# Weight pieces split into high and low parts in two halves, with TensorE waiting per half piece

## What is computed

```python
def swiglu(h, w_gu, w_down):
    gate, up = jnp.split(h @ w_gu, 2, axis=-1)
    return (jax.nn.silu(gate) * up) @ w_down
...
x = x + 0.5 * swiglu(rmsnorm(x, ffn1_norm[i]), ffn1_w_gu[i], ffn1_w_down[i])
```

## Time and profile before

| | |
|---|---|
| median of three runs | 3886.77 us |
| the profiled execution's own time | 3886.8 us |
| its span, first to last instruction | 3885.0 us |
| mean granted TensorE clock | 0.958 |
| TensorE busy | 3564.5 us (92%) |
| VectorE busy | 2276.5 us (59%) |
| ScalarE busy | 1839.1 us (47%) |
| GpSimd busy | 606.9 us (16%) |

### The profile page before, as it was taken

One profiled execution on the slowest core, in us unless ns is written; L12 is line 12 of the kernel. 1 busy time (PEld: TensorE's weight loads), 2 busy tenths in 40 slices (PEclk: granted clock), 3 DMA queues, 4 the chain that ended last, 5 costly groups with the idle time before them and its releaser, 6 DMA issues. The chain is left out here.

```text
span 3885.0 us, 45081 instructions
## 1 busy us (share of the span) xinstructions
PE 3564.5 (92%) x18342; PEld 2997.1 (77%) x18342; DVE 2276.5 (59%) x2608; ACT 1839.1 (47%) x2400; POOL 606.9 (16%) x208
## 2 busy tenths in 40 slices
PE   7998799999899996899998799899998789999999
PEld 6887677788778876688887688787878568787887
DVE  4475458776566667656666454555555554555654
ACT  4453257665356562456554244444443344444443
POOL 0001129572042320142400200000000000000000
PEclk9998899999999998899998899999999899999999
DMA  5542046665276752376743035454544115354453
GB/s 217 188 148 87 1 174 239 225 240 204 101 271 233 275 206 106 134 258 238 265 166 131 1 109 189 153 189 149 198 163 164 62 68 194 142 200 157 152 195 136
DMA packets 89978, 653.57 MB, mean 168 GB/s; under 512 B 10032, under 2 KB 10032, under 8 KB 10928
## 3 DMA queue, kind: packets, MB, share of 16 engines
q1 hardware_dynamic: 78768, 573.10, 40.4%
q0 software_dynamic: 11008, 77.60, 5.6%
HBM read 649.61 MB, written 1.05 MB: 167 GB/s over the span
## 5 line engine op out<-in xcount | busy, mean ns | idle before, releaser
L1424 DVE TENSOR_TENSOR w_lo<-raw,w_hi 128x2048 fp32r<-128x2048 f32 x540 | 1421.0, 2636 | 661.0 <-ACT w_hi L1003 660.7
L1003 ACT ACTIVATE w_hi<-raw 128x2048 fp32r<-128x2048 f32 x540 | 1031.0, 1913 | 601.2 <-PE acc L518 410.2
L516 PE MATMUL wrk<-w_hi,h_hi 128*128 128x512 f32 (+1 forms) x2496 | 973.3, 390 | 61.5 <-DVE w_lo L1424 41.4
L518 PE MATMUL wrk<-w_hi,h_lo 128*128 128x512 f32 (+1 forms) x2496 | 956.2, 383 | 0.0
L517 PE MATMUL wrk<-w_lo,h_hi 128*128 128x512 f32 (+1 forms) x2496 | 955.1, 383 | 0.0
L516 PEld LDWEIGHTS wrk<-w_hi,h_hi 128*128 128x128 f32 x2496 | 473.7, 190 | 157.8 <-DVE w_lo L1424 52.3
L2082 POOL TENSOR_TENSOR arena<-arena,c 128x2048 f32<-128x2048 f32 x92 | 492.1, 5356 | 473.1 <-ACT arena L1003 447.1
L518 PEld LDWEIGHTS wrk<-w_hi,h_lo 128*128 128x128 f32 x2496 | 472.9, 189 | 93.3
L517 PEld LDWEIGHTS wrk<-w_lo,h_hi 128*128 128x128 f32 x2496 | 474.0, 190 | 85.2 <-issue 0.2
L516 PE MATMUL acc<-w_hi,hid_hi 128*128 128x512 f32 x1144 | 447.9, 392 | 9.4 <-DVE hid_lo L1507 9.4
L518 PE MATMUL acc<-w_hi,hid_lo 128*128 128x512 f32 x1144 | 445.9, 390 | 0.0
(11 more groups left out here) (254 smaller groups left out, 3501.4 us busy)
## 6 DMA issues: line engine op xcount, KB each, us to landing
raw<-in_wts SPq DMA_DIRECT2D x540, 1024.0 KB, 4.8
arena<-in_mods POOLq DMA_DIRECT2D x72, 1024.0 KB, 5.2
const<-in_const SPq DMA_DIRECT2D x1, 2176.0 KB, 10.1
c<-in_bias POOLq DMA_DIRECT2D x8, 256.0 KB, 3.4
x<-in_x SPq DMA_DIRECT2D x1, 1024.0 KB, 5.3
c<-in_c SPq DMA_DIRECT2D x1, 1024.0 KB, 4.8
out<-x SPq DMA_DIRECT2D x1, 1024.0 KB, 3.9
row<-in_rows SPq DMA_DIRECT2D x1, 512.0 KB, 11.5
```

The costliest lines, as they stand in the source:

```text
L516: nc.tensor.matmul(o, l_h, r_h, start=first, stop=False, skip_group_check=True)
L518: return nc.tensor.matmul(o, l_l, r_h, start=False, stop=last, skip_group_check=True)
L1003: return nc.scalar.activation(o, i, f, **kw)
L1424: tt(w_lo[:, ns % SLOTS, :], raw[:, ns % SLOTS, :], w_hi[:, ns % SLOTS, :].bitcast(F32), ALU.subtract).then_inc(lo_ready, 1)
```

## The change

`hi` and `lo` each issue two instructions of 128 x 1024 for a piece instead of one of 128 x 2048, and `hi_ready` and `lo_ready` count two per piece. TensorE's wait moves from the head of each call to the first product that uses a half (`split(n, part)`). The load of piece n waits until both halves of piece n - 3 are split, as before. `grouped` still waits for the whole piece. The matmuls, their order and the loads are the same.

```diff
             def load(n):
                 if n >= SLOTS:
-                    sp.wait_ge(lo_ready, n - SLOTS + 1)
+                    sp.wait_ge(lo_ready, 2 * (n - SLOTS + 1))
...
+            def split(n, part):
+                pe.wait_ge(lo_ready, 2 * n + part + 1)
...
             def across(ns, o, h_at=None, n_at=None, kc=KC):
-                pe.wait_ge(lo_ready, ns + 1)
                 s = ns % SLOTS
                 for q in range(kc):
+                    if q % 4 == 0:
+                        split(ns, q // 4)
...
                 def gate_up(s, p, t):
                     n = ns + (3 * s - 1 if s else 0) + p
-                    pe.wait_ge(lo_ready, n + 1)
...
                     for q in range(4):
+                        if q % 2 == 0:
+                            split(n, q // 2)
...
                 def down(s, t, half):
-                    pe.wait_ge(lo_ready, n + 1)
                     pe.wait_ge(taken, use[name, f"t{s}"] + 1)
                     for j in range(2):
+                        split(n, j)
...
                 def part(n, t, wait=False):
-                    pe.wait_ge(lo_ready, ns + n + 1)
                     for q in range(4):
+                        if q % 2 == 0:
+                            split(ns + n, q // 2)
...
                 def grouped(ns, kc, k0, width, labels, h_at=None, along_=False):
-                    pe.wait_ge(lo_ready, ns + 1)
+                    split(ns, 1)
...
-                fn(w_hi[:, ns % SLOTS, :], raw[:, ns % SLOTS, :], ACT.Copy).then_inc(hi_ready, 1)
+                for part in range(2):
+                    v = slice(part * PW // 2, (part + 1) * PW // 2)
+                    fn(w_hi[:, ns % SLOTS, v], raw[:, ns % SLOTS, v], ACT.Copy).then_inc(hi_ready, 1)
...
             def lo(ns):
-                dve.wait_ge(hi_ready, ns + 1)
-                tt(w_lo[:, ns % SLOTS, :], raw[:, ns % SLOTS, :], w_hi[:, ns % SLOTS, :].bitcast(F32),
-                   ALU.subtract).then_inc(lo_ready, 1)
+                for part in range(2):
+                    dve.wait_ge(hi_ready, 2 * ns + part + 1)
+                    v = slice(part * PW // 2, (part + 1) * PW // 2)
+                    tt(w_lo[:, ns % SLOTS, v], raw[:, ns % SLOTS, v], w_hi[:, ns % SLOTS, v].bitcast(F32),
+                       ALU.subtract).then_inc(lo_ready, 1)
```

## The result

A ratio compares a kernel's runs with those of the kernel before on the same chip; it lies near the ratio of the two medians, but is not exactly that (at most 0.001 apart).

The account below looks back on a forecast made before the run. TensorE, busy 92% of the span, was taken as the bound. The terms sum to -8.8 us, and with -6.9 of clock to -15.7, taking 3886.8 to 3871.1 us; the range was 3860 to 3893.

Parts of the forecast that it names:

- start: Start of the program: VectorE starts piece 0 1.07 us earlier, taken as -0.9 us because TensorE is at half clock.
- five modulated openings and the clock behind them: Five modulated FFN openings: each TensorE wait loses 1.07 us, -5.3; behind three, the lost clock all returns, -6.9 us.
- delta-net projections: Two mixers: TensorE's 0.19 us wait for `w_lo` at every second piece, 12 times, goes: -2.3 us.
- stick-breaking and sparse mixer; splits in chains: Sparse mixer between -1 and +1, taken as -0.2 us; extra split time ahead of chains in mixers and FFNs, +1.7 us.
- attention: Second attention opening: the piece ahead of `turned_low` ends at 2949.9 instead of 2950.6, -0.6 us.
- GpSimd openings, `ffn2_0`: Opening of `ffn2_0`: the second GpSimd product gets between the halves and delays the second half, +2.1 us.
- `ffn2_1`, and the three like `ffn1_2`: Openings: in `ffn2_1` the first half precedes the product, -2.3 us; in `ffn1_2` and its like a wait goes, -1.25 each.
- steps of `ffn2_0`: Steps where VectorE and GpSimd alternate without pause: 0.15 us for each of 27 pieces, +4.0 us.
- `ffn1_1`, its opening and steps: Opening with the same pattern as `ffn1_2`, -1.25 us; its steps only in the range, up to +10 if drawn in.
- rival B: Whole kernel: waits shrink but the 1.2 GHz stretches stay, 3878 us; chance 0.22.
- rival C: GpSimd products between halves stall TensorE 3.0 us each in mid-piece; with 12 stalls 3907 us, slower; chance 0.15.

Follow-up runs that it names:

- second trace: The changed kernel run once more with no edit, for a second profile: 3900.41 us, ratio 1.004.
- run 1: The changed kernel with pieces split whole in the six FFNs with GpSimd products, halves elsewhere: 3879.42 us, ratio 0.9987.
- run 11: The changed kernel with each GpSimd product cut into four of 128 x 512, back to back: 3873.38 us, ratio 0.9966.
- run 9: The changed kernel with halves only in the first two pieces of FFNs without GpSimd products and in delta-net and attention mixers: 3876.55 us, ratio 0.9982.
- run 6: The changed kernel with whole pieces in `ffn2_0` and `ffn1_1` alone, halves everywhere else: 3879.03 us, ratio 0.999.
- runs 4 and 5: The kernel before and the changed kernel, each with GpSimd products replaced by fills of zeros: 3857.34 and 3847.01 us.
- run 12: The kernel before, whole pieces, with each GpSimd product cut into four of 128 x 512: 3914.53 us, ratio 1.0074.
- run 7: The changed kernel with halves on ScalarE only; VectorE's part is one instruction that waits for both: 3900.95 us, ratio 1.0052.

## Why the prediction was wrong, step by step

Stage by stage, of the profiled executions (us, after minus before; a stage ends with its last update of `x`), by the prediction's own terms. The stages are read from unrounded times and add up to the 7.4 us; the forecast was -15.7:

| term | predicted | measured |
|---|---|---|
| start | -0.9 | longest wait for `w_lo` 12.5 to 11.6; stage -2.2, second trace +0.3 |
| five modulated openings and the clock behind them | -5.3 and -6.9 | five stages: -5.1 |
| delta-net projections | -2.3 | waits gone; two stages -1.6 and +3.1 |
| stick-breaking and sparse mixer; splits in chains | -0.2 and +1.7 | +2.0 and -0.2 |
| attention | -0.6 | -0.8 |
| GpSimd openings, `ffn2_0` | +2.1 | +4.2 |
| `ffn2_1`, and the three like `ffn1_2` | -2.3, and -1.25 each | -1.6, and -0.2, -0.1, +1.4 |
| steps of `ffn2_0` | +4.0 | +4.3 |
| `ffn1_1`, its opening and steps | -1.25 | +4.0 |

**Right.** The sizes of the halves. A met wait costs nothing that these rows show: steps of after, with 16 waits for pieces instead of 8 (the prediction says 12 calls a step; its own count of matmuls, four calls of 12 and four of 6, makes 8), in the chain of waits,

```profile
3207.79 0.44 PE wrk L618 x4
...
3224.57 0.44 PE wrk L618 x4
```

stand 16.78 us apart as before. The start, the attention opening, and the waits of 0.19 in the projections, of which none is left, though the second delta-net mixer as a whole came out longer (below).

**The openings, mis-sized.** Four of the five waits are 1 us shorter, as the earlier trace rows let expect, the fifth is not:

```profile
2715.00 0.47 PE L520 MATMUL wrk<-w_hi,h_hi 128*128 128x512 f32 x1 [2.32 <-DVE w_lo L1436]
...
3703.71 0.47 PE L520 MATMUL wrk<-w_hi,h_hi 128*128 128x512 f32 x1 [2.35 <-DVE w_lo L1436]
```

```profile
2715.10:2721.80 6.70, 6.70 (x23) 5.35 (x24) 3.58 (x4) 1.10 (x2) 0.00 (x0) 0.75 0.71 267
3695.10:3698.50 3.40, 3.40 (x12) 2.74 (x11) 2.46 (x11) 0.00 (x0) 0.00 (x0) 0.50 0.00 0
```

The second fence is two windows. In the first, behind a wait that was 3.3 us, the granted clock is 0.75, where it was 0.50 over 6.7 us: half of the stretch at 1.2 GHz is gone, not all. The nearest rows, the two waits of 2.4 us, did not carry over, though the waits became 2.3. The second window lies in the fifth opening, behind idle time of 2.02 us that the kernel before had too (2.07), at full clock there; it delays the transposes and takes the gain. Behind the first of the three waits, the one of 3.4 us at 0.50, nothing came back (0.59 at 2516.9 to 2520.3). By TensorE's busy time in these stages 2.1 of the 6.9 us of clock came, 0.8 and 1.3, and 1.4 went in the fifth stage. So the openings came nearer to rival B than to the forecast.

**GpSimd openings.** In `ffn1_2` the wait of 1.30 went, as forecast, though because both halves ran ahead of the product and not with the product between them. But "the next one (0.46) about stays" was wrong: DVE, POOL and PE of after,

```profile
1277.35 6.13 DVE L1436 TENSOR_TENSOR w_lo<-raw,w_hi 128x1024 fp32r<-128x1024 f32 x1 [0.46 <-ACT w_hi L1011]
...
1277.77 4.61 POOL L2094 TENSOR_TENSOR arena<-arena,c 128x2048 f32<-128x2048 f32 x1
...
1283.53 0.50 PE L520 MATMUL wrk<-w_hi,h_hi 128*128 128x512 f32 x1 [1.80 <-DVE w_lo L1436]
```

The next product held the first half of the next piece, and the wait for it is 1.80: 1.76 us of waits are now 1.80, and the two FFNs like it fare the same (1.63 to 1.78, 1.75 to 1.79). In the second of these, `ffn1_3`, the granted clock was 0.50 for 3.4 us behind the wait, where it had been full; that is its +1.4. `ffn2_1` did gain, 1.6 us. In `ffn2_0` the product got between the halves as forecast; TensorE waited 3.13 us at 538.29, and behind it the granted clock was 0.50, where before it was full; the 2.1 us did not hold that. The window:

```profile
537.80:541.20 3.40, 2.91 (x7) 2.33 (x8) 3.40 (x5) 0.29 (x1) 0.24 (x1) 0.51 0.71 222
```

**Clock outside the openings.** The forecast had no term for it. The second delta-net mixer is 3.1 us longer, with its idle time as before (43.4 us in both). After, and before:

```profile
2000.60:2305.90 305.30, 261.85 (x1760) 234.15 (x1761) 176.99 (x344) 122.70 (x224) 28.24 (x12) 0.89 0.20 73
...
1990.50:2292.60 302.10, 258.66 (x1760) 230.69 (x1761) 175.61 (x322) 120.95 (x203) 28.25 (x12) 0.90 0.20 74
```

The stick-breaking mixer's +2.0 is of the same kind (1.8 of it busy time). The halves in the mixer do not settle it alone: with the same halves it took 299.8 us in run 1, 300.4 in run 11 and 300.0 in run 9, and 305.3 in both traces of after.

**The steps, where the sign was decided.** The forecast priced one product against one pair of halves, and put only the second instruction's fixed cost (0.15 us for each of 27 pieces) on the path of `ffn2_0`. "The total of GpSimd's time, all that can block, doesn't grow" was the argument against rival C. It is true, and GpSimd's time even fell, but it is the wrong sum. While both engines had work queued they took turns in these stages, one instruction each: a whole piece and a product in 6.7 us before, half a piece and a product in 5.6 us now. VectorE gets half as much done per turn, so a piece takes two turns, some 11 us, while products last. It falls behind, and TensorE is stopped in mid-piece. The +4.3 us of the steps has the size of the forecast, +4.0, by accident: it is mostly two stalls of 3.35 and one wait of 5.95 us where three of 1.5 to 1.6 and one of 3.2 had been, and not 27 times 0.15. `ffn1_1` was held to be safe by VectorE's lead ("up to +10 if `ffn1_1` is drawn in too" was kept in the range only); the lead goes in two turns.

So two steps of the prediction failed. A product against halves was priced at 0.15 us a piece and with `ffn1_1` safe: `ffn2_0` and `ffn1_1` were to take 4.9 us more and took 12.5, of which 9.3 are idle time of TensorE. And all of the 6.9 us of clock was to come back: TensorE's matmul time rose by 7.4 us instead. Of the 23.1 us between forecast and trace, 7.7 lie in these two FFNs, 7.1 in the modulated openings with their clock, 5.6 in the other GpSimd openings and 3.8 in the delta-net mixers. With the two FFNs whole (run 6) the gain is 5.5 us, not the 20.6 that the other terms of the forecast add up to.

**Rival C** is what happened in the two FFNs, and B in most of the rest, with clock lost besides. A stall was priced at 3.0 us and takes 3.35; there are three in steps, not twelve, and the openings and `hid_lo` add to them. The rule of the Trainium skill (SBUF — State Buffer, "Who interferes with whom"), that such a VectorE instruction and a GpSimd instruction that reads SBUF exclude each other, is borne out by runs 4 and 5: with fills, which read nothing of SBUF, no subtraction took over 2.44 us, not even where a fill ran beside it. The same section of the Trainium skill says that issue order decides who blocks; here it was seen not to be enough, since in run 12 a piece stood behind products that started after it.

What stays open: what decides where the granted clock falls, in run 7 above all, and what makes GpSimd give way or not. The 5 us by which the medians of before and after differ more than their profiled executions fit the clock too, without being shown to be it: the six runs of after go from 3894.2 us at a mean clock of 0.956 to 3903.8 at 0.952.

## What to carry to other kernels

Where two engines exclude each other and both have work queued, price an edit per turn and not per instruction: cutting one engine's instruction in two halves what it gets per turn, unless the other's are cut as well. Here the same halves cost 12 to 16 us beside long products, gain 10 without them and give the lowest median (3873.4 us) beside short ones. Do such a split only in the stages that wait for it and don't share, and count little of the clock that a wait might give back when it shrinks without vanishing: here 2.1 of 6.9 us came. With the same matmuls, read busy and idle time of TensorE apart: the first is the clock, the second the waits.

## What was not expected of the hardware

A VectorE instruction can be held by many GpSimd instructions in a row: 12.6 us at most in run 12 (min/median/max in ns),

```profile
L1424 DVE TENSOR_TENSOR w_lo<-raw,w_hi x540: 2276/2293/12642, 24.8 to 3887.1; 128x2048 fp32r<-128x2048 f32 x180
```

through short products of 1.25 us each, against 6.9 for one long product in the kernel before. The short ones alone have made the kernel before 29 us slower. And the granted clock fell at 3695 behind a wait of 2.02 us in after, but not behind the same wait, 2.07 us, in before: one wait's length did not decide it.
